# Stick-breaking heads moved between the steps of the triangular inverses, whose first and last level make fewer products

## What is computed

```python
# delta rule (the reference solves 64-row chunks; the kernel inverts 128 x 128 systems: 8 heads x 2 halves)
lmat = jnp.where(strict, beta[..., :, None] * kk * decay, 0.0)
amat = lmat + jnp.eye(DN_CHUNK)
sol = lax.linalg.triangular_solve(amat, rhs, left_side=True, lower=True, unit_diagonal=True)

# stick breaking: A[t,s] = beta[t,s] prod_{s<j<t}(1-beta[t,j]), beta = sigmoid(q.k/sqrt(Dh)), s<t
z = jnp.einsum('bqhd,bkhd->bhqk', q_blk, kf) * scale
log_rem = jnp.where(causal, jax.nn.log_sigmoid(-z), 0.0)
after = lax.cumsum(log_rem, axis=3, reverse=True) - log_rem
attn = jnp.where(causal, jnp.exp(jax.nn.log_sigmoid(z) + after), 0.0)
o_sb = jnp.einsum('bhqk,bkhd->bqhd', attn, vf)

# both branches are projected up, gated, added and projected again
y_dn = o.reshape(B, S, DN_V) @ w_up_dn
y_sb = o_sb.reshape(B, S, SB_W) @ w_up_sb
out = (g_dn * y_dn + g_sb * y_sb) @ w_out
```

## Time and profile before

| | us |
|---|---|
| median of three runs | 4221.89 |
| the profiled execution, its own time | 4238.3 |
| its span in the trace | 4236.4 |
| PE busy | 3801.3 |
| DVE busy | 2458.3 |
| ACT busy | 1851.6 |

### The profile page before, as it was taken

One profiled execution on the slowest core, in us unless ns is written; L12 is line 12 of the kernel. 1 busy time (PEld: TensorE's weight loads), 2 busy tenths in 40 slices (PEclk: granted clock), 3 DMA queues, 4 the chain that ended last, 5 costly groups with the idle time before them and its releaser, 6 DMA issues. The chain is left out here.

```text
span 4236.4 us, 54665 instructions
## 1 busy us (share of the span) xinstructions
PE 3801.3 (90%) x21553; PEld 3272.0 (77%) x21553; DVE 2458.3 (58%) x3041; ACT 1851.6 (44%) x1978; POOL 53.4 (1%) x27
## 2 busy tenths in 40 slices
PE   5988789988887789999999986997687999999999
PEld 4968569988685667778877775994477999877887
DVE  6636325566362258888888843634413887455665
ACT  3521513444215156776766633532212444433554
POOL 0000000000000000000000000000000000000000
PEclk9978799989797899999999997996588999857999
DMA  6640026557300269999999952450022555302554
GB/s 223 240 153 5 1 109 222 187 178 257 107 1 20 80 219 360 362 363 362 366 362 361 363 188 93 160 180 10 6 90 100 163 181 182 110 1 69 193 192 161
DMA packets 296869, 739.06 MB, mean 174 GB/s; under 512 B 17449, under 2 KB 17904, under 8 KB 291312
## 3 DMA queue, kind: packets, MB, share of 16 engines
q1 hardware_dynamic: 296688, 736.60, 49.3%
HBM read 735.50 MB, written 1.05 MB: 174 GB/s over the span
## 5 line engine op out<-in xcount | busy, mean ns | idle before, releaser
L1877 DVE TENSOR_TENSOR weight_ring_low<-weight_ring,weights_high 128x2048 fp32r<-128x2048 f32 x336 | 773.5, 2344 | 149.5 <-ACT weights_high L1823 149.5
L1823 ACT ACTIVATE weights_high<-weight_ring 128x2048 fp32r<-128x2048 f32 x336 | 618.3, 1907 | 6.9 <-DMA weight_ring<-in_moe_w 6.9
L374 PE MATMUL psum_all<-h_high_projections,high_projections 128*128 128x256 f32 x1536 | 448.9, 292 | 62.9 <-DVE weight_ring_low L429 37.3
L374 PE MATMUL psum_all<-h_low_projections,high_projections 128*128 128x256 f32 x1536 | 444.3, 289 | 0.0
L374 PE MATMUL psum_all<-h_high_projections,weight_ring_low 128*128 128x256 f32 x1536 | 440.0, 286 | 0.0
L1765 PE MATMUL psum_all<-weights_high,expert_in_turn_high 128*128 128x512 f32 x896 | 359.6, 401 | 17.8 <-DVE weight_ring_low L1877 11.6
L1765 PE MATMUL psum_all<-weights_high,expert_in_turn_low 128*128 128x512 f32 x896 | 356.8, 398 | 0.0
L374 PEld LDWEIGHTS psum_all<-h_high_projections,high_projections 128*128 128x128 f32 x1536 | 301.2, 196 | 68.0 <-issue 37.9
L1765 PE MATMUL psum_all<-weight_ring_low,expert_in_turn_high 128*128 128x512 f32 x896 | 352.2, 393 | 0.0
L374 PEld LDWEIGHTS psum_all<-h_high_projections,weight_ring_low 128*128 128x128 f32 x1536 | 304.5, 198 | 0.0
L374 PEld LDWEIGHTS psum_all<-h_low_projections,high_projections 128*128 128x128 f32 x1536 | 302.4, 197 | 0.0
(11 more groups left out here) (572 smaller groups left out, 7957.9 us busy)
## 6 DMA issues: line engine op xcount, KB each, us to landing
weight_ring<-in_moe_w SPq DMA_DIRECT2D x336, 1024.0 KB, 5.1
weight_ring<-in_w_in SPq DMA_DIRECT2D x48, 2048.0 KB, 8.8
expert_rows<-in_peer_down SPq DMA_DIRECT2D x128, 512.0 KB, 3.3
expert_rows<-in_peer_up SPq DMA_DIRECT2D x128, 512.0 KB, 3.3
weight_ring<-in_ffn_halves SPq DMA_DIRECT2D x42, 1024.0 KB, 6.1
branch_out<-in_ada_w SPq DMA_DIRECT2D x64, 512.0 KB, 6.3
weight_ring<-in_w_out SPq DMA_DIRECT2D x6, 2048.0 KB, 7.7
weight_ring<-in_ada_w SPq DMA_DIRECT2D x4, 2048.0 KB, 11.6
```

The source lines that it names most:

```text
L374: mm = pe.matmul(half(k.ps, 4 * (g % R) + j), w[:, c, j * P:(j + 1) * P], x[:, c], start=(c == 0 and n == 0), stop=(c == KC - 1 and n == 2))
L1823: act.activation(high[:, q, h * HALF:(h + 1) * HALF], k.ring[:, q, h * HALF:(h + 1) * HALF], ACT.Copy).then_inc(high_made[q], 1)
L1877: dve.tensor_tensor(k.low[:, q, part], k.ring[:, q, part], high[:, q, part].bitcast(F32), ALU.subtract).then_inc(low_made[q], 1)
```

## The change

The stages `sb_turn` and `sb_heads` are gone. A class `StickBreaking` holds their operations, and `delta_inverse` calls it on each engine: `turn` and `values` at the start, and `tensor(n)`, `vector(n)` and `scalar(n)` at the end of step n. The heads are spread over the 28 steps. Scores come in steps 0 to 7, Ln in three batches in steps 8 to 10, `sums` in the even steps 10 to 24, `mix` in the odd steps 13 to 27. The scaling of the scores passes from DVE to ACT. The heads use PSUM banks 6 and 7. Their tiles `z`, `e`, `at` and `vt` now lie in the three slots of `k.ring`, so that the ring can't hold the next weights meanwhile: `projections` is called with `ahead=0` and stops issuing at its own panels, and the three panels for `branches` are issued by SP in `delta_outputs`. The output of the heads goes to `k.proj[:, SQ0 + j]`.

In the inverse, the first level (steps 0 to 3) starts from the identity: the right product takes `k.ident` in place of `xi`, there are no copies of the identity at the start, no copy to `px` and no both products; DVE computes identity minus the bank for `xi` and identity minus `mt` for `xt`. In the last level (steps 24 to 27) only `xt` is updated, and only its product is made. DVE's `mask` waits for the update before it.

```diff
-            started, masked, right, copied, both, updated = st.signals(6)
+            masked, right, copied, both, updated = st.signals(5)
+            sb.begin(st.signals(14))
+            N = 28
+            LAST = N - 4
...
-                for g in range(4):
-                    for x in (xi, xt):
-                        dve.tensor_copy(x[:, g], row_bc(k.ident, 4)).then_inc(started, 1)
                 def mask(n):
                     if n >= 4:
                         dve.wait_ge(right, n - 4 + 1)
+                        dve.wait_ge(updated, updates(n - 4))
...
+                    if n < 4:
+                        dve.wait_ge(right, n + 1)
+                        dve.tensor_tensor(xi[:, g], ident, bank(g % 2), ALU.subtract).then_inc(updated, 1)
+                        dve.wait_ge(masked, n + 1)
+                        dve.tensor_tensor(xt[:, g], ident, mt[:, g], ALU.subtract).then_inc(updated, 1)
+                    else:
+                        dve.wait_ge(both, n - 4 + 1)
+                        dve.wait_ge(updated, updates(n - 4))
+                        if n < LAST:
+                            dve.tensor_tensor(xi[:, g], xi[:, g], bank(b), ALU.subtract).then_inc(updated, 1)
+                        dve.tensor_tensor(xt[:, g], xt[:, g], bank(b + 1), ALU.subtract).then_inc(updated, 1)
+                    if n + 4 < N:
                         mask(n + 4)
+                    sb.vector(dve, n)
...
+                    if n < LAST:
+                        for e in range(4):
+                            pe.matmul(bank(b)[:, e], xt[:, g, e], px[:, g, e], start=True, stop=True)
                     for e in range(4):
                         mm = pe.matmul(bank(b + 1)[:, e], px[:, g, e], xt[:, g, e], start=True, stop=True)
...
+                sb.turn(pe)
+                for n in range(N + 1):
+                    if n < N:
                         right_product(n)
-                    if n >= 1:
+                    if n >= 5:
                         both_products(n - 1)
+                    sb.tensor(pe, n)
...
+            @block.sync
+            def _(sp):
+                k.issue(sp, k.start[f"up_dn{l}"] + R)
...
+    def tensor(self, pe, n):
+
+        if n < self.H:
+            self.scores(pe, n)
+        if n >= 10 and n % 2 == 0 and (n - 10) // 2 < self.H:
+            self.sums(pe, (n - 10) // 2)
+        if n >= 13 and n % 2 == 1 and (n - 13) // 2 < self.H:
+            self.mix(pe, (n - 13) // 2)
...
+    def vector(self, dve, n):
...
+        h = n - 8
+        if 0 <= h < self.H:
+            dve.wait_ge(self.logged, h + 1)
+            s = self.e[:, h]
+            dve.scalar_tensor_tensor(s, self.z[:, h], 0.0, s, ALU.max, ALU.add).then_inc(self.joined, 1)
...
+        h = (n - 9) // 2
+        if n % 2 == 1 and 0 <= h < self.H:
+            dve.wait_ge(self.summed, h + 1)
...
+    def scalar(self, act, n):
...
+        if h < self.H:
+            s = self.e[:, h]
+            act.wait_ge(self.scored, h + 1)
+            act.activation(self.z[:, h], self.bank(h % 2)[:, 0:self.W], ACT.Copy, scale=64 ** -0.5).then_inc(self.z_ready, 1)
...
+        for h in range(3 * (n - 8), min(3 * (n - 8) + 3, self.H)) if n >= 8 else ():
+            act.wait_ge(self.grown, 2 * h + 2)
+            act.activation(self.e[:, h], self.e[:, h], ACT.Ln, bias=1.0).then_inc(self.logged, 1)
+        h = (n - 12) // 2
+        if n % 2 == 0 and 0 <= h < self.H:
+            act.wait_ge(self.shifted, h + 1)
+            act.activation(self.at[:, h], self.z[:, h], ACT.Exp).then_inc(self.attn, 1)
...
-                            k.h, k.proj, conv=(0, 6, f"conv{l}", None), extra=extra)
+                            k.h, k.proj, ahead=0, conv=(0, 6, f"conv{l}", None), extra=extra)
                 delta_rule(k, l)
-                stick_breaking(k, l)
```

More of the change, by code:

```diff
@@ L1024, in both_products @@
                     g = n % 4
[L1025 to L1027 removed]
+                    pe.wait_ge(copied, n - 4 + 1)
+                    if n >= 6:
+                        pe.wait_ge(updated, updates(n - 2))
                     b = 2 + 2 * (g % 2)
[L1029 to L1030 removed]
+                    if n < LAST:
+                        for e in range(4):
+                            pe.matmul(bank(b)[:, e], xt[:, g, e], px[:, g, e], start=True, stop=True)
                     for e in range(4):
@@ new lines, in bank, with turn, values @@
+    def bank(self, i):
+        return self.k.ps[:, 6 + i, :]
+    def turn(self, pe):
+        for i in range(TT):
+            for b in range(4):
+                mm = pe.transpose(self.bank(i)[:, b * P:(b + 1) * P], self.k.proj[:, SV0 + b, i * P:(i + 1) * P], self.k.ident)
+            mm.then_inc(self.turned, 1)
+    def values(self, act):
+        for i in range(TT):
+            act.wait_ge(self.turned, i + 1)
+            act.activation(self.vt[:, i], self.bank(i), ACT.Copy).then_inc(self.valued, 1)
@@ new lines, in scores @@
+    def scores(self, pe, h):
+        k, W = self.k, self.W
+        if h < 2:
+            pe.wait_ge(self.valued, h + 1)
+        else:
+            pe.wait_ge(self.z_ready, h - 1)
+        rows, b = slice(64 * (h % 2), 64 * (h % 2) + 64), h // 2
+        o = self.bank(h % 2)
+        pe.matmul(o[:, 0:T], k.proj[rows, SK0 + b, 0:P], k.proj[rows, SQ0 + b, :], start=True, stop=True)
+        pe.matmul(o[:, T:W], k.proj[rows, SK0 + b, P:T], k.proj[rows, SQ0 + b, P:T], start=True, stop=True).then_inc(self.scored, 1)
@@ new lines, in sums @@
+    def sums(self, pe, h):
+        k, W = self.k, self.W
+        pe.wait_ge(self.summed_in, h + 1)
+        if h >= 1:
+            pe.wait_ge(self.shifted, h)
+        o, s = self.bank(0), self.e[:, h]
+        pe.matmul(o[:, 0:T], k.tri_ge, s[:, 0:T], start=True, stop=False, skip_group_check=True)
+        pe.matmul(o[:, P:T], k.ones, s[:, T:W], start=False, stop=True, skip_group_check=True)
+        pe.matmul(o[:, T:W], k.tri_ge, s[:, T:W], start=True, stop=True, skip_group_check=True).then_inc(self.summed, 1)
@@ new lines, in mix @@
+    def mix(self, pe, h):
+        j, W = h // 2, self.W
+        pe.wait_ge(self.attn, h + 1)
+        if j >= 1 and h % 2 == 0:
+            pe.wait_ge(self.taken, j)
+        r0 = 64 * (h % 2)
+        o = self.bank(1)[r0:r0 + 64, 0:T]
+        pe.matmul(o, self.vt[:, 0, 64 * h:64 * h + 64], self.at[:, h, 0:T], start=True, stop=False, skip_group_check=True)
+        pe.matmul(o[:, P:T], self.vt[:, 1, 64 * h:64 * h + 64], self.at[:, h, T:W], start=False, stop=True, skip_group_check=True).then_inc(self.mixed, 1)
@@ L1324, in _ @@
             def _(pe):
-                for i, (panels, src0) in enumerate(parts):
+                for i, (panels, src) in enumerate(parts):
                     if i >= 2:
```

182 lines of the change are left out of this document (55 added, 127 removed).

## The result

| | before | after |
|---|---|---|
| median of 4 runs, us | 4224.70 (4219.86 to 4232.13) | 4168.68 (4164.28 to 4179.07) |
| profiled execution, its span | 4236.4 | 4177.3 |
| PE busy | 3801.3 | 3778.9 |
| DVE busy | 2458.3 | 2441.1 |
| ACT busy | 1851.6 | 1813.8 |

The ratio of after to before is 0.9869, with a 95% interval of 0.9845 to 0.9894: faster by 56 us. The forecast was 4147, 75 us less than before. 4168.68 lies just within the range of 4128 to 4170, and outside the likeliest case's own range of 4139 to 4158. The direction was right, the size too large by a third, and that is what the experiments had to explain.

What follows compares the result with a forecast made beforehand. The inverse was taken to be bound by PE, the heads' stages to be serial time; the terms summed to -37.4 us a layer, -74.8 for both, taken off the median 4221.9 for 4147, range 4128 to 4170.

Steps and rivals of the forecast that it cites:

- the likeliest case: Whole kernel: the forecast of 4147 us itself, own range 4139 to 4158, chance 0.65.
- the second rival: Inverse with heads: queues hold each other, each head costing PE about 1.5 us, 12 a layer; 4171 us, chance 0.15.
- The two stages go: From the first transpose of `sb_turn` to the first matmul of `branches`: serial time removed, -48.5 us a layer.
- Products that are not made: First and last level of the inverse: 96 matmul instructions fewer on PE, -10.7 us a layer.
- the start: Start of the inverse: PE no longer waits for the copies of the identity, -3.4 us a layer.
- The heads' matmuls: Inverse: scores, sums and mix add 2.71 us of PE time for each of 8 heads, +21.7 us a layer.
- The start of the inverse at half clock: First steps of the inverse: half clock for some 5.5 us as before, so no term in the sum.
- The rival of the half clock: Inverse: waits between groups keep PE at clock 0.50, +47 us a layer; 4315 us, chance 0.03.
- The wait at `sums(0)`: Inverse, after step 8: PE waits once for DVE's `second(0)`, +0.4 us a layer.
- DVE and ACT otherwise: Inverse steps with heads: DVE's lag and ACT's two table loads stay within PE's slack and cost nothing.
- The end: End of the inverse: DVE makes one update after the last product in place of two, -0.6 us a layer.
- The ring: Panels for `branches` issued when `delta_outputs` starts: they land within 35.7 us, so 0.

Runs made afterwards that it cites:

- paired_scores: Changed kernel with the scores of two heads made behind each other in steps 0, 2, 4 and 6; 4141.18 us, 0.9800 of the kernel before.
- warm_late: `late_scores` plus unneeded matmuls, five before `delta_inverse`, two and three in `delta_norm`; 4144.88 us, 0.9805 of the kernel before.
- late_scores: Changed kernel with no scores in steps 0 to 4, two heads' scores in each of steps 5 to 8; 4138.96 us, 0.9788 of the kernel before.
- warm_inverse: Changed kernel with five unneeded 512-column matmuls at the end of `delta_products`; 4147.34 us, 0.9817 of the kernel before.

## Why the prediction was right, and where its sum was off

The forecast of 4147 was 22 us too low, and the total fell in the stated range because that range was widened towards the second rival, whose mechanism did not occur. So the range was hit in part by luck; of the terms, all but the one of the half clock held to within 1.6 us a layer. Two of the signs that the prediction named failed with that term: the clock was to be 1.00 from some 6 us on and was so from 23, and `delta_outputs` was to begin 91.5 us after PE's first start and began 101.1 after it.

**The two stages go, -48.5.** Measured -48.5. A serial stage that reads nothing of its neighbours is worth its length between two barriers, and this was the best supported term.

**Products that are not made, -10.7, and the start, -3.4.** Borne out. A step of the last level without heads is 451.37 - 449.58 = 1.79 us in the changed kernel, two products of 0.893 in place of three, and PE begins at 354.28 where DVE begins at 354.27.

**The heads' matmuls, +21.7.** Measured 2.91 a head in place of 2.71, +23.3. The sums were cheaper than their row (0.88 for 1.07; behind a product they have no gap), the scores and the mix dearer by 0.2 each: to the start of what follows they take their 0.85 and 0.80, but the product ahead of the mix takes 405.32 - 404.33 = 0.99 in place of 0.89 and the one behind it 407.11 - 406.12 = 0.99 again. The rows of before had no product next to these groups. So a price read between two rows need not hold beside other neighbours.

**The start of the inverse at half clock, of before's length.** This is the step that failed. The text says "that stretch is in the 78 us of before, and I expect one of the same length". It was 23 us and not 5.5, and lost 10.7 us instead of 2.75: +7.9 a layer, 15.8 of the 19.9 us that the stretches of the two layers saved less than the sum (54.9 against 74.8). The reasoning asked only whether the first steps keep PE *occupied* (1.73 us of work a step against 1.9 of DVE) and not what they fill it with. The rival of the half clock had the right place and the wrong trigger: it was argued from waits between groups and put aside because PE's load only rises. PE's load was full (99.61 of 101 us), there were no waits, and the clock stayed low. Of "TensorE: Matmul & The Clock Gate", the page of the Trainium skill that stood behind this rival, the section "What's actually happening" has the warm-up as a matter of time and not of the number of matmuls; the runs here disagree, with 6 us of half clock in `paired_scores` and 23 in the changed kernel behind the same barrier, where PE has the same work in another order.

**The wait at `sums(0)`, +0.4.** Measured 0.42, at 395.33, behind the DVE operation that was named.

**DVE and ACT otherwise, 0.** Borne out: no other row of PE from 378 to the end of the stage waits for more than the gaps of its small groups. Two table loads stand in the stage, as forecast; the timeline of ACT in the changed kernel:

```profile
388.82 1.28 ACT L1309 ACT_TABLE_LOAD   x1
390.11 1.35 ACT L1309 ACTIVATE weight_ring<-weight_ring 128x384 f32<-128x384 f32 x3
...
400.70 1.28 ACT L1313 ACT_TABLE_LOAD   x1
401.99 0.52 ACT L1313 ACTIVATE weight_ring<-weight_ring 128x384 f32<-128x384 f32 x1
```

So the rival of queues that hold each other fell, though its time (4171) is within 3 us of the measured one. The time alone would have borne it out, the trace does not.

**The end, -0.6.** Measured -0.5: from the last product of the inverse to `delta_outputs` it is 455.36 - 453.15 = 2.21 where it was 2.71.

**The ring, 0.** Borne out. The DMA issues of the changed kernel from 450 to 500 us, which answer to the earlier trace rows:

```profile
weight_ring<-in_w_up_dn SPq DMA_DIRECT2D x2, 2048.0 KB, 11.3
weight_ring<-in_w_up_sb SPq DMA_DIRECT2D x1, 2048.0 KB, 18.4
```

Issued from 455.32 on, right behind each other, they take longer to land than before (8.8 and 7.6), and the last, issued at 456.37, is there some 17 us ahead of `branches`.

**The clock of `branches`, +2.8.** Measured +2.5: the window from 491.8 has a clock of 0.50 and the next 0.67. The stretch from `delta_outputs` to `branches` took 0.8 us more (36.5 for 35.7), which the sum didn't have.

Added up for a layer: -37.4 + 7.9 + 1.6 + 0.1 + 0.8 - 0.3 = -27.3, and the trace has -27.5.

What stays open is which trait of the single 64-row scores went with the long half clock, the empty rows or the gaps: 128-row scores also lose their gaps, pairs also give PE twice the instructions in a group, and no kernel changed the rows and nothing else. Each of these clocks was read from one profiled execution of its kernel; in all of them the inverse took the same in both layers, to 0.1 us, while the stretches behind it differed between the layers by up to 3 us in two (`warm_late`, `paired_scores`).

## What to carry to other kernels

When work is added to a pipelined stage, look at what the tensor engine gets in the first microseconds after a barrier, and not only at whether it is busy: a thin but unbroken stream ran for 23 us at half clock here, and the same stream entered at full clock kept it. Three remedies worked here: full-height matmuls first (`late_scores`), half-height ones in pairs in the two halves of the rows (`paired_scores`), and unneeded matmuls where the tensor engine is idle before the barrier (`warm_inverse`). The first two add no work. Measure such a price by stage and by trace before believing the total, since a rival's time can match for the wrong reason.

## What the hardware showed that was not expected

- Half clock with PE busy all the time: 0.50 with 3.00 of 3.00 us busy, for 23 us, and 6 us with 128-row or paired scores. The same stream, entered at 1.00, ran at 1.00 throughout.
- The scores of two heads in different halves of the rows lengthen a step by 1.05 us, those of one head by 1.04.
- A group of 64-row or 64-column matmuls lengthens the product on each side of it by 0.1 us (0.99 for 0.89).
- Unneeded matmuls in time that PE would idle away took 10.7 us a layer off the stage behind them.
